# Scores without the product of beta and a: the inner product reads the block products' off-diagonal blocks instead

## What is computed

```
sa = einsum('bhij,bhj->bhi', s, -kk_t)
s = (s * w_t + sa[..., None] * (kk_t * a_t) + v_t[..., None] * k_t)
y = einsum('bhij,bhj->bhi', s, r_t)
```

## Time and profile before

| | |
|---|---|
| median of 3 runs | 2315.65 us (2315.08 to 2320.18) |
| the profiled execution, its own time | 2314.71 us |
| its span, first to last instruction | 2312.9 us |
| TensorE busy | 2242.7 us, 97% |
| VectorE, ScalarE, GpSimd busy | 62%, 55%, 25% |
| mean granted TensorE clock | 0.993 |

### The profile page before, as it was taken

One profiled execution on the slowest core, in us unless ns is written; L12 is line 12 of the kernel. 1 busy time (PEld: TensorE's weight loads), 2 busy tenths in 40 slices (PEclk: granted clock), 3 DMA queues, 4 the chain that ended last, 5 costly groups with the idle time before them and its releaser, 6 DMA issues.

```text
span 2312.9 us, 72365 instructions
## 1 busy us (share of the span) xinstructions
PE 2242.7 (97%) x31109; PEld 1706.9 (74%) x31109; DVE 1445.5 (62%) x2699; ACT 1279.8 (55%) x2757; POOL 578.9 (25%) x1070
## 2 busy tenths in 40 slices
PE   7999999999999999889999999999999998999998
PEld 5777777777777776777888888888888886544443
DVE  6444554544455555567777777777777777456675
ACT  7455555555555545645666666666666665343333
POOL 0000000000000000355455555556556555100000
PEclk9999999999999999999999999999999999999999
DMA  6112222222333331222222232322232335566665
GB/s 245 69 56 70 80 79 87 82 79 79 100 116 118 107 101 49 53 58 68 70 77 78 82 87 79 85 57 77 82 87 81 86 86 147 186 231 217 219 236 182
DMA packets 217278, 244.62 MB, mean 106 GB/s; under 512 B 110080, under 2 KB 159552, under 8 KB 212608
## 3 DMA queue, kind: packets, MB, share of 16 engines
q1 hardware_dynamic: 211056, 217.44, 30.5%
q10 hardware_dynamic: 5904, 22.55, 2.7%
HBM read 141.83 MB, written 98.10 MB: 104 GB/s over the span
## 4 chain that ended last, share of the span: by engine, by line
PE 42%; POOL 6%; DVE 4%; DMA 3%; issue 2%; ACT 1%; SPq 1%; DVEq 0%; ACTq 0%
PE first L2125 14%; PE first L2417 8%; PE r_d L2125 5%; POOL r_inv L2086 3%; POOL r_inv_tmp L2084 3%; PE r_d L2417 2%; PE r_AB L2219 2%; PE r_EO L2325 1%; PE r_EO L2342 1%; PE r_AB L2230 1%; PE r_EO L2286 1%; PE r_EO L2303 1%; DMA scratch_inverse<-r_inv 1%; PE first L2193 1%; PE r_AB L2272 1%
## 5 line engine op out<-in xcount | busy, mean ns | idle before, releaser
L2125 PE MATMUL first<-h,w_hi 128*128 128x256 f16 (+1 forms) x2496 | 420.8, 273 | 0.0
L2084 POOL TENSOR_TENSOR r_inv_tmp<-r_inv 64x30 f32<-64x30 f32 (+14 forms) x480 | 266.3, 555 | 417.9 <-DMA r_inv<-scratch_blocks 381.5
L748 PE MATMUL d<-h,w_hi 128*128 128x256 f16 (+1 forms) x2176 | 353.6, 271 | 0.0
L2125 PE MATMUL first<-h,w_lo 128*128 128x256 f16 (+1 forms) x1248 | 339.3, 273 | 0.0
L748 PE MATMUL d<-h,w_lo 128*128 128x256 f16 (+1 forms) x1088 | 293.0, 271 | 0.0
L2086 POOL TENSOR_TENSOR r_inv<-r_inv,r_inv_tmp 64x30 f32<-64x30 f32 (+14 forms) x480 | 280.1, 584 | 37.6
L2125 PEld LDWEIGHTS first<-h,w_hi 128*128 128x128 f16 x2496 | 238.7, 98 | 50.5 <-issue 18.9
L748 PEld LDWEIGHTS d<-h,w_hi 128*128 128x128 f16 x2176 | 211.2, 99 | 32.7 <-issue 3.5
L2027 POOL MEMSET r_run_s<- 128x128 f16 x1 | 0.2, 205 | 918.5 <-POOLq L390 918.5
L748 PE MATMUL first<-h,w_hi 128*128 128x256 f16 (+1 forms) x1168 | 184.8, 268 | 5.0 <-DVE w_lo L1236 3.1
L2125 PE MATMUL r_d<-h,w_hi 128*128 128x256 f16 (+1 forms) x960 | 159.6, 272 | 0.5 <-DVE carry_s L2756 0.5
(11 more groups left out here) (393 smaller groups left out, 5112.0 us busy)
## 6 DMA issues: line engine op xcount, KB each, us to landing
h<-in_x SPq DMA_DIRECT2D x33, 512.0 KB, 3.8
r_ops<-in_x SPq DMA_DIRECT2D x33, 512.0 KB, 4.0
out_y<-r_ops SPq DMA_DIRECT2D x33, 512.0 KB, 7.7
scratch_hT<-h SPq DMA_DIRECT2D x16, 1024.0 KB, 7.1
h<-scratch_hT ACTq DMA_DIRECT2D x15, 1024.0 KB, 7.0
scratch_mg<-m_hl SPq DMA_DIRECT2D x33, 256.0 KB, 2.0
r_zr<-scratch_zr SPq DMA_DIRECT2D x33, 256.0 KB, 3.6
r_bon<-scratch_bonus SPq DMA_DIRECT2D x33, 256.0 KB, 4.9
```

The lines of the kernel that those rows point to most:

```text
L748: mm = pe.matmul(out, lhs(k, a, w), rhs(k, a, w), start=(n == 0), stop=(n == len(terms) - 1))
L2084: step(pool.tensor_tensor(tmp, inv[0:n, 0:u, u:u + 1].to_broadcast([n, u, w]), inv[0:n, u:u + 1, u + 1:32].to_broadcast([n, u, w]), ALU.mult))
L2125: mm = pe.matmul(out, lhs(k, a, w), rhs(k, a, w), start=(m == 0), stop=(m == 3 * KT - 1))
```

## The change

For the blocks of the prompt (b of 1 or more) `scores` leaves out beta'a: the eight products of beta have N = 64 (r alone) in place of 128. The products of kappa keep N = 128. The `inner` product takes beta'a from `xb`, where it stands already masked: of each matrix the block of rows 0 to 31 and columns 32 to 63, which SyncE copies to the rows where the inner product reads it, into a new part `xo` of `bu_all`. There are four such copies for a block, of 32 rows x 8 matrices x 32 numbers each. They are issued between the inverse's store and the wait for its landing, behind a wait for the last inner product of the block before, and raise the semaphore that `td` waits for. The inner product becomes a product of 32 x 32 with 32 columns, on four tiles of the array. In block 0 nothing of this changes, but its T1 is loaded by eight smaller transfers, so that the semaphore counts to 8 there too.

```diff
-        bu_all = sb("bu", [P, 2 * 1024 + 384])
+        bu_all = sb("bu", [P, 2 * 1024 + 512])
...
+        xo = bu_all[:, 2048:2560].rearrange("p (c g t) -> p c g t", c=4, g=4)
...
-        t1_in = sig("first_blocks_in", 4, NB, 16)
+        t1_in = sig("first_blocks_in", 8, NB, 16)
...
                 sp.dma_start(packed(y_d, b), inv[0:16 * nc_, :, :]).then_inc(*y_back.up(b))
+                if b:
+                    sp.wait_ge(w_full.sem, w_full.at(last_chunk(b - 1), 1))
+                    for h in range(2):
+                        for a in range(2):
+                            k = 64 * swapped(h, a)
+                            sp.dma_start(xo[64 * h:64 * h + 32].rearrange("s c (g a) t -> s a (c g) t", a=2)[:, a],
+                                         xb[k:k + 32, :, :, 32:64].rearrange("s c (g a) t -> s a (c g) t", a=2)[:, a])\
+                              .then_inc(*t1_in.up(b))
                 sp.wait_ge(y_back.sem, y_back.at(b, 1))
...
-                        sp.dma_start(T1[64 * h:64 * h + 32, 0:nc_].rearrange("s c (g a) t -> s a (c g) t", a=2)[:, a],
-                                     blocks[a]).then_inc(*t1_in.up(b))
+                        for c0, c1 in ((0, nc_),) if b else ((0, 1), (1, 2)):
+                            sp.dma_start(T1[64 * h:64 * h + 32, c0:c1].rearrange("s c (g a) t -> s a (c g) t", a=2)[:, a],
+                                         blocks[a][:, 2 * c0:2 * c1]).then_inc(*t1_in.up(b))
...
-                        yield h, bk[hrows(half_)], ops[hrows(h), b % 3, p, g, cols]
+                        yield h, p, bk[hrows(half_)], ops[hrows(h), b % 3, p, g, cols]
...
-                    for h, out, src in stack(b, ch, g):
-                        mm = pe.matmul(out[:, g * P:(g + 1) * P], src, ops[hrows(h), b % 3, A_:R_ + 1, g, cols],
-                                       start=True, stop=True)
+                    for h, src_plane, out, src in stack(b, ch, g):
+                        if b and src_plane == T_:
+                            mm = pe.matmul(out[:, g * P + CH:(g + 1) * P], src, ops[hrows(h), b % 3, R_, g, cols],
+                                           start=True, stop=True)
+                        else:
+                            mm = pe.matmul(out[:, g * P:(g + 1) * P], src, ops[hrows(h), b % 3, A_:R_ + 1, g, cols],
+                                           start=True, stop=True)
...
                         c0 = 384 + (g // 2) * 32
+                        if b:
+                            r0, r1 = 64 * h, 64 * swapped(h, g) + 32
+                            mm = pe.matmul(EO[r1:r1 + 32, h, c0:c0 + 32], xo[r0:r0 + 32, ch, g, :],
+                                           TD[r0:r0 + 32, ch, g, :], start=True, stop=True, tile_position=(r0, r1))
+                            continue
...
-                dve.wait_ge(t1_in.sem, t1_in.at(b, 4))
+                dve.wait_ge(t1_in.sem, t1_in.at(b, 8))
```

More of the change, by code:

```diff
@@ L2228, in turn @@
                 for g in range(4):
-                    for h, out, src in stack(b, ch, g):
+                    for h, _, out, src in stack(b, ch, g):
                         pe.matmul(out[:, g * CH:(g + 1) * CH], src, ident2[hrows(h), :], start=True, stop=True)
```

## The result

| | median, us | lowest to highest |
|---|---|---|
| before, 11 runs | 2316.41 | 2309.51 to 2322.12 |
| after, 11 runs | 2325.52 | 2320.85 to 2333.10 |

After over before is 1.0042, interval 1.0026 to 1.0058: the kernel became 9 to 10 us slower, where 3.2 were forecast. The time lies just inside the range (2305 to 2326), but the cause is the second rival, "T1 comes late", and not the forecast. The profiled execution of after has 2331.85 us of its own, 6.3 above its median, and 17.1 above the profiled one of before, so its totals overstate the change by about 8 us.

The account below looks back on a forecast made before the run. TensorE and the inverse's loop were taken as about equally long bounds. Scores 0, inner 2.2 and copies 1 summed to 3.2 us on 2314.7, giving 2317.9 to 2318.9, said as 2318.5 us; range 2305 to 2326.

Parts of the forecast that it names:

- T1 comes late: Slower rival: the copies outlast the store and T1 lands 0.6 us or more later per block; above 2325 us, chance 0.15.
- What bounds the kernel: Second phase: TensorE, 98% busy, and the inverse's loop, 62.8 us a block, are about equally long.
- Scores, 0: Scores step on TensorE: the two tiles with kappa still stream eight 128-column records, so 0 us saved per chunk.
- the signal of beta's last product may come earlier: End of the scores step: an earlier signal to VectorE was thought possible, worth 0 as VectorE is not the bound.
- Inner, +2.2: Inner product: nothing won behind a projection piece, 0.16 us lost behind head sums, 14 times: 2.2 us slower.
- The copies, +1: SyncE's queue, between store and its landing: four copies hidden by 0.7 us; 0.1 us in nine blocks, 1 us slower.
- if nothing hides them: Upper bound for the copies: 1.81 us in 9 waiting blocks and 0.7 in 7 others, 21 us.
- The faster rival: The rival "The shorter products count", on TensorE's scores: gain capped by the inverse's loop, 2306 us, chance 0.2.
- The chances: Odds for the whole kernel's time: faster 0.22, same (about 0.2%) 0.45, slower 0.33.
- The shorter products count: Faster rival, scores: rounds go by all columns, saving 0.20 us for 64 chunks, 13 us; priced at 2306, chance 0.2.
- Inner on four tiles is no faster than on two: Slower rival, inner product: 0.12 us more in each of 64 chunks, 7.7 us on top of 2.2; 2325 us, chance 0.15.
- the second sign: Timeline sign of "T1 comes late": T1's transfers start over 3.1 us behind the store's issue, transpose waits exceed 12 us.

Follow-up runs that it names:

- wide_scores: After, with all 16 products of scores at N = 128 again; 2324.37 us, 1.0041 over before.
- balanced: early_copies with beta and kappa changing tiles for odd g, so every tile gets four records of 64 and four of 128 columns; timing only; 2312.26 us, 0.9991 over before.
- all_short: early_copies with kappa's products at 64 columns too, leaving part of the scores out; timing only; 2318.14 us, 1.0000 over before.
- small_inner: Before, with only the inner product in the new 32 x 32 form, read from the masked scores, no copies; 2319.37 us, 1.0009 over before.
- early_copies: After, with its four copies moved up SyncE's list, ahead of the store of the part before (put_m:0); 2320.88 us, 1.0018 over before.
- copies_only: After, with scores and inner as in before; the copies are made and nothing reads them; 2330.06 us, 1.0054 over before.

## Why the prediction missed

- **What bounds the kernel**: right, and the part that carries the rest. The inverse's loop is as long as TensorE's work. About 1.1 us more on the path cost 0.5 to 0.9 us a block, and 16 us less on TensorE brought 4, though there the lower clock had a part too.
- **Scores, 0**: right. wide_scores equals after, and balanced and all_short show why: a step lasts as long as its longest tile. The guess that the signal of beta's last product may come earlier was wrong, and cost nothing.
- **Inner, +2.2**: borne out in its parts (0.25 us to unknowns in both places, and an entry of 0.31 instead of 0.20 behind the head sums, medians of the 15 steps that stand there; the forecast counted 14), and small_inner's +2.1 agrees, with an interval that just includes 0. The Trainium skill's rule in the page TensorEngine Tiling (Array Packing) (Tiling Modes, Key Properties), that a change of mode drains the engine, agrees with that entry.
- **The copies, +1**: this is the step that failed. I took a copy to issue like a transfer into T1, 0.45 us, and so four of them to be "hidden by 0.7 us". The cover was read rightly, 38.3 us over 15 blocks, 2.55 each. The copies need 4 x 0.63 and their gaps, 2.66 and more where one stalls. They overrun, and T1's transfers then lost their short issue as well (2.68 us for the four instead of 1.81), which the forecast did not think of and which is the larger part of the 1.1 us. The term measured 5.6 us from after to early_copies; what copies_only lost in all is 1.0054 - 1 = 12.5 us, with an interval of 8.6 to 16.2.
- **The place of the error in the reasoning**: I had the price "if nothing hides them" in my bounds, and from 1.81 us at that. The durations of issue were the one thing that the trace of before did not show for this kind of transfer, and I took the nearest row without its own uncertainty. 40% more on it was enough. Four issues of 0.63 us are 0.7 us more than four of 0.45, as much as the whole margin. The rival "T1 comes late" hung on that margin and was given 0.15.
- **The rivals' prices**: two of the sums were off. 9 x 0.6 to 16 x 0.6 on top of 2317.9 is 2323.3 to 2327.5, so "above 2325" holds for the upper half only. The faster rival was capped at 8 us "and a bit" and then priced at 12.
- **The chances**: slower 0.33 was too low, within 0.2% at 0.45 too high. "The shorter products count" and "Inner on four tiles is no faster than on two" are both shown wrong, the latter by 0.25 where it had 0.37.
- **What would show it**: the second sign was the right one. T1's transfers start 3.29 us behind the store, beyond the 3.1 that I had named, and the waits of the transpose are 22.1, beyond 12.

The measured sum: 2.1 (small_inner) and 5.6 (copies' place) make 7.7 of the 9.7 us that 1.0042 stands for. The other 2 would be what early_copies keeps over small_inner (1.0018 against 1.0009). The waiting copies ahead of `put_m:0` may be it, but their intervals overlap, and it stays open. Open too: why copies_only lies above after; why an issue of this kind takes 0.63 us; and whether a version with balanced scores and their results moved to where the next steps read them would gain. It was not tried; balanced, which leaves out that work, is 2 us under before with an interval that includes none, so little is left for it. Of the versions that compute everything, none was faster than before.

## What to carry to other kernels

A wait for a transfer that lands is free room on its queue only up to its length, and how long a new kind of transfer takes to issue is to be put in with a wide bound where the margin is thin: here 0.18 us more for each of four, and the slower issues behind them, decided between free and 6 us. Where two chains of work are about equally long, a saving on one brings little (4 of 16 us here) and a delay on either is paid for the most part, so a change to one should leave the other untouched. Shorter products on some tiles of the array save nothing until every tile is shorter: balance the columns over the tiles first.

## What the hardware showed unexpectedly

- A copy within the fast memory, 32 rows of eight pieces of 32 numbers, took 0.63 us of SyncE's queue (median of 64), and a transfer from HBM of the same shape 0.45 (medians in after's and before's lines).
- Four tiles of 64 x 64 go on independently: a step of 16 products took 0.787 us from the first to the last start with all short records on two tiles, 0.632 with them spread, and 0.435 with all short. This is the Trainium skill's rule in the page TensorEngine Tiling (Array Packing) (Tiling Modes, Key Properties), that different tiles work in parallel.
- Starts on different tiles do not keep the order of the program, but the signal does. In after the last product of the step started 0.22 us before earlier ones of kappa, and VectorE, which waits for its semaphore, started 0.33 us behind the last start of kappa, as before. The Trainium skill's page TensorE: Matmul & The Clock Gate (Part 3, The mechanism) has products start and end strictly in program order. For the starts this trace decides against it; for the end the signal agrees.
- The clock: granted 0.99 in the second phase of after against 1.00 before, in an execution that was itself 6.3 us above its median. It is not the main cause of the loss. At the same granted clock of 0.992 and on one chip, before took 2316.0 us (mean of 13 runs) and wide_scores, which is as slow as after, 2324.3 (5 runs). No experiment changed the clock alone, so whether it followed the longer idle gaps or added to them stays open.
